# One scan for the four state sequences of a pair, the backward direction kept in scan order, output weights of power zero copied

## The reference

```python
for direction in range(2):
    lam_bar = jnp.exp(lam * dt)                      # complex, 32 groups x 64 states
    b_bar = ((lam_bar - 1.0) / lam)[..., None] * (b_re + 1j * b_im)
    order = (lambda t: t) if direction == 0 else (lambda t: jnp.flip(t, axis=1))
    bu_c = einsum('gpk,blgk->blgp', b_bar, order(uc))
    x_c = ssm_scan(lam_bar, bu_c)                    # x[t] = lam_bar * x[t-1] + bu[t]
    bu_l = einsum('gpk,blgk->blgp', b_bar, order(ul))
    bu_l = bu_l.at[:, 0].add(lam_bar * x_c[:, -1])   # latents go on from the context's last state
    x_l = ssm_scan(lam_bar, bu_l)
    ys_l += order(einsum('gkp,blgp->blgk', c_mat, x_l).real)
    ys_c += order(einsum('gkp,blgp->blgk', c_mat, x_c).real)
y = gelu(ys + d * u); y = y * sigmoid(y @ glu_w + glu_b)
```

## Time and profile before

| | |
|---|---|
| median of 3 runs | 1921.41 us (1920.11 to 1926.1) |
| the profiled execution | 1922.82 us, its span 1921.0 us |
| PE busy, share of the span | 1833.4 us, 95% |
| DVE | 1220.0 us, 64% |
| ACT | 728.3 us, 38% |
| POOL | 62.6 us, 3% |
| DMA | 257.81 MB, mean 134 GB/s |
| mean granted clock of PE | 0.969 |

### The profile page before, as it was taken

One profiled execution on the slowest core, in us unless ns is written; L12 is line 12 of the kernel. 1 busy time (PEld: TensorE's weight loads), 2 busy tenths in 40 slices (PEclk: granted clock), 3 DMA queues, 4 the chain that ended last, 5 costly groups with the idle time before them and its releaser, 6 DMA issues.

```text
span 1921.0 us, 25350 instructions
## 1 busy us (share of the span) xinstructions
PE 1833.4 (95%) x9680; PEld 1539.9 (80%) x9680; DVE 1220.0 (64%) x2020; ACT 728.3 (38%) x1003; POOL 62.6 (3%) x39
## 2 busy tenths in 40 slices
PE   6899999999889799999999999999999999989998
PEld 2688888877788587888888878888888797789998
DVE  4677677778999854777577357766333434755554
ACT  2522122336766833322132252312322434654343
POOL 0000000020000001000000100000002000010001
PEclk7999999999989998999999999999999999989999
DMA  7444545331110122554464235444223241034553
GB/s 298 154 175 157 188 183 209 120 113 66 45 45 28 39 72 104 186 202 148 148 235 146 94 129 192 172 153 178 95 77 113 107 176 55 2 111 174 179 183 120
DMA packets 39860, 257.81 MB, mean 134 GB/s; under 512 B 4688, under 2 KB 5840, under 8 KB 14832
## 3 DMA queue, kind: packets, MB, share of 16 engines
q1 hardware_dynamic: 39792, 256.92, 37.1%
HBM read 255.85 MB, written 1.05 MB: 134 GB/s over the span
## 4 chain that ended last, share of the span: by engine, by line
PE 84%; DVE 10%; ACT 3%; issue 2%; DMA 1%; SPq 0%; DVEq 0%; ACTq 0%
PE ps_all L1574 26%; PE ps_all L1578 25%; PE ps_all L1575 25%; DVE w_lo L924 2%; PE ps_all L1964 2%; PE bank L1622 1%; DMA start_scale<-in_w_scale 1%; PE bank L1977 1%; PE bank L2000 1%; ACT w_hi L538 1%; DVE cp L432 1%; DVE stat L1307 1%; PE bank L1789 1%; DVE wb L1238 0%; DVE normed L1294 0%
## 5 line engine op out<-in xcount | busy, mean ns | idle before, releaser
L1574 PE MATMUL ps_all<-a_hi,w_lo 128*128 128x512 f32 (+1 forms) x1800 | 663.4, 369 | 21.5 <-ACT a_hi L648 14.0
L1578 PE MATMUL ps_all<-a_lo,w_hi 128*128 128x512 f32 (+1 forms) x1800 | 657.4, 365 | 0.2 <-DVE a_lo L1063 0.2
L1575 PE MATMUL ps_all<-a_hi,w_hi 128*128 128x512 f32 (+1 forms) x1800 | 657.2, 365 | 0.0
L924 DVE TENSOR_TENSOR w_lo<-w_raw,w_hi 128x2048 fp32r<-128x2048 f32 (+3 forms) x184 | 376.5, 2046 | 162.1 <-ACT w_hi L538 160.9
L538 ACT ACTIVATE w_hi<-w_raw 128x2048 fp32r<-128x2048 f32 (+3 forms) x183 | 313.5, 1713 | 338.4 <-PE ps_all L1578 331.0
L1574 PEld LDWEIGHTS ps_all<-a_hi,w_lo 128*128 128x128 f32 x1800 | 345.5, 192 | 79.7 <-issue 16.2
L1578 PEld LDWEIGHTS ps_all<-a_lo,w_hi 128*128 128x128 f32 x1800 | 345.2, 192 | 56.8 <-DVE a_lo L1063 4.1
L1575 PEld LDWEIGHTS ps_all<-a_hi,w_hi 128*128 128x128 f32 x1800 | 345.8, 192 | 52.1 <-issue 0.2
L936 DVE SCALAR_TENSOR_TENSOR mod_junk<-mod_raw,cond 128x1024 bf16<-128x1024 f32 x256 | 302.7, 1220 | 5.4 <-ACT cond L566 2.7
L1574 PE MATMUL ps_all<-g_hi,w_lo 128*128 128x512 f32 (+1 forms) x704 | 258.4, 367 | 1.0 <-DVE w_lo L924 1.0
L1578 PE MATMUL ps_all<-g_lo,w_hi 128*128 128x512 f32 (+1 forms) x704 | 258.3, 367 | 0.0
(11 more groups left out here) (236 smaller groups left out, 1512.0 us busy)
## 6 DMA issues: line engine op xcount, KB each, us to landing
w_raw<-in_tiles SPq DMA_DIRECT2D x118, 1024.0 KB, 4.8
mod_raw<-in_w_mod SPq DMA_DIRECT2D x64, 1024.0 KB, 4.8
w_raw<-in_tiles SPq DMA_DIRECT2D x32, 768.0 KB, 4.1
w_raw<-in_tiles SPq DMA_DIRECT2D x32, 640.0 KB, 3.7
start_raw<-in_w_mod SPq DMA_DIRECT2D x4, 1024.0 KB, 16.1
start_scale<-in_w_scale SPq DMA_DIRECT2D x4, 1024.0 KB, 20.2
bias<-in_na_bias SPq DMA_DIRECT2D x2, 1536.0 KB, 8.9
cond<-in_cond SPq DMA_DIRECT2D x2, 1024.0 KB, 6.0
```

What stands on the lines that cost most here:

```text
L924: nc.vector.tensor_tensor(w_lo[:, slot, 0:size], w_raw[:, slot, 0:size], w_hi[:, slot, 0:size].bitcast(F32), ALU.subtract).then_inc(lo_rea ...
L1574: pe.matmul(dst, w[1], x[0], start=start, stop=False)
L1575: pe.matmul(dst, w[0], x[0], start=False, stop=False)
L1578: return pe.matmul(dst, w[0], x[1], start=False, stop=stop_)
```

## The change

- **Scans.** One `tensor_tensor_scan` over 512 elements does all four sequences of a pair. Its factors come from a new tile `rates` (two slots), which holds the rate of the direction in columns 1 to 127 of each sequence and zero in column 0, so that each sequence starts anew. POOL writes the zeros once, ACT writes the rest for each pair (`scan_rates`), and DVE waits for it.
- **Order of the backward direction.** For this the backward sequences have to lie in the order in which they are scanned. PE gets the blocks of `us` reversed within each half for the two backward products of `inputs_to_state`, and the backward states reversed in `outputs` (`in_scan_order`). The step numbers are then the same for both directions, and `const` is 128 columns narrower. `xs` is 129 columns for each sequence, with the padding in front.
- **States.** `turn_back` writes them with one instruction for each part instead of two.
- **Output weights.** `c_products` and `c_combine` do powers 1 to 4 only. Power zero is C itself (its imaginary part negated): ACT copies it into slots 0 and 9 (`present_outputs`), and `kernel_products` waits for that. All four products now lie in `prod`; `rates` takes the place of `cprod` and of a gap.

```diff
-    c[:, C_STEP:C_STEP + 2 * P] = np.concatenate(
-        [np.arange(1, P + 1), np.arange(64, 0, -1), np.arange(P, 64, -1)])
+    c[:, C_STEP:C_STEP + P] = np.arange(1, P + 1)
...
+                def present_outputs(b):
+                    act.wait_ge(S["pads"], 1)
+                    if b >= 2:
+                        act.wait_ge(S["y"], 2 * b - 2)
+                    for ri in range(2):
+                        for g in range(2):
+                            at = slice(64 * g, 64 * g + 64)
+                            ins = nc.scalar.activation(cp[at, b % 2, :, ri, 0::9, 16 * g:16 * g + 16],
+                                                       c_in[at, ri, 4 * b:4 * b + 4, :].rearrange("p (q d) k -> p q d k", d=2),
+                                                       ACT.Copy, scale=1.0 if ri == 0 else -1.0)
+                    ins.then_inc(S["present"], 1)
+                def scan_rates(pair):
+                    if pair >= 2:
+                        act.wait_ge(S["scan"], pair - 1)
+                    for d in range(2):
+                        ins = nc.scalar.activation(rates[:, pair % 2, d, :, 1:P],
+                                                   ones[:, 1:P].rearrange("p (a j) -> p a j", a=1).broadcast_to([P, 2, P - 1]), ACT.Copy,
+                                                   scale=r4[:, 2 * pair + d:2 * pair + d + 1])
+                    ins.then_inc(S["rates"], 1)
...
                 angles(0)
+                present_outputs(0)
+                scan_rates(0)
+                scan_rates(1)
                 split_hi(base + 1, 2048, 1)
...
                         angles(b + 1)
+                        present_outputs(b + 1)
                         turned(2 * b + 2)
                         turned(2 * b + 3)
...
+                    if b < 7:
+                        scan_rates(2 * b + 2)
                     gelu(2 * b)
                     if b < 7:
                         sines(b + 1)
+                        scan_rates(2 * b + 3)
...
-                    to = [prod[:, 320 * n:320 * n + 320] for n in range(2)] + [cprod[:, n] for n in range(2)]
+                    to = [prod[:, 256 * n:256 * n + 256] for n in range(4)]
...
-                    for ri in range(2):
-                        ins = nc.vector.tensor_tensor_scan(zs[:, 1, ri, 63::-1], r[1].broadcast_to([P, 64]),
-                                                           rot[:, 0, 1, ri, 63::-1], 0.0, mul, add)
-                    ins.then_inc(S["half"], 1)
-                    for ri in range(2):
-                        nc.vector.tensor_tensor_scan(zs[:, 0, ri, :], r[0].broadcast_to([P, P]),
-                                                     rot[:, 0, 0, ri, :], 0.0, mul, add)
-                    dve.wait_ge(S["half"], pair + 1)
-                    for ri in range(2):
-                        ins = nc.vector.tensor_tensor_scan(zs[:, 1, ri, 127:63:-1], r[1].broadcast_to([P, 64]),
-                                                           rot[:, 0, 1, ri, 127:63:-1], zs[:, 1, ri, 0:1], mul, add)
-                    ins.then_inc(S["scan"], 1)
+                    dve.wait_ge(S["rates"], pair + 1)
+                    nc.vector.tensor_tensor_scan(sq_acc[:], rates[:, slot].rearrange("p d r j -> p (d r j)"), scaled[:, 0],
+                                                 0.0, mul, add).then_inc(S["scan"], 1)
...
                     for ri, op in ((0, sub), (1, add)):
-                        at, to = ri * P + 63, ri * 130 + 65
-                        b = [back[:, n].rearrange("p d r j -> p (d r j)")[:, at:at + 194:193] for n in range(2)]
-                        nc.vector.tensor_tensor(flat[:, to:to + XS_D + 65:XS_D + 64], b[0], b[1], op)
-                        x_to = x[:, :, ri * 130:ri * 130 + 130].rearrange("p d (b j) -> p d b j", b=2)[:, :, :, 0:64]
-                        ins = nc.vector.tensor_tensor(x_to, back[:, 0, :, ri, :], back[:, 1, :, ri, :], op)
+                        ins = nc.vector.tensor_tensor(xs[:, pair % 2, :, ri, 1:P + 1], back[:, 0, :, ri, :], back[:, 1, :, ri, :], op)
...
+                nc.gpsimd.memset(rates[:, :, :, :, 0:1], 0.0)
...
+                def in_scan_order(x, d):
+                    return x.rearrange("p (b j) -> p b j", b=2)[:, :, ::-1] if d else x
...
-                        mm = pe.matmul(bank[1 + pair % 2][:, n * P:(n + 1) * P], vt[:, pair % 2, n, :], us_of(pair),
+                        mm = pe.matmul(bank[1 + pair % 2][:, n * P:(n + 1) * P], vt[:, pair % 2, n, :], in_scan_order(us[:, pair, :], n // 2),
...
                     pe.wait_ge(S["c"], b + 1)
+                    pe.wait_ge(S["present"], b + 1)
...
-                            x = xs[:, slot, XS_D * d + 130 * ri:XS_D * d + 130 * ri + 130].rearrange("p (b j) -> p b j", b=2)[:, :, d:d + 64]
-                            mm = pe.matmul(o, lhs, x, start=False, stop=(d == 1 and ri == 1))
+                            mm = pe.matmul(o, lhs, in_scan_order(xs[:, slot, d, ri, 0:P], d), start=False, stop=(d == 1 and ri == 1))
```

More of the change, by code:

```diff
@@ L75 @@
 COLUMNS = 2 * CHUNKS + 76
-XS_D = 262
 MAGIC = 1.5 * 2 ** 23
@@ L266, in program @@
                 prod = sbuf("prod", [P, 1024], F32, s5)
-                cprod = sbuf("cprod", [P, 2, 320], F32, s5)
-                sbuf("between", [P, 5632 - 4 * 1024 - 512 - 640], F32, s5)
+                rates = sbuf("rates", [P, 2, 2, 2, P], F32, s5)
                 c_in = sbuf("c_in", [P, 2, 32, 16], F32, s5)
@@ L326, in program @@
         s5_sem = {n: sem("s5_" + n) for n in (
-            "rows", "loads", "skip", "act", "tanh", "sin", "b", "pads", "us_act", "wprod", "w", "cprod", "c",
-            "ang", "magic", "frac", "abs", "tables", "turned", "vt", "v", "kmm", "k", "rot", "z", "half", "scan",
+            "rows", "loads", "skip", "act", "tanh", "sin", "b", "pads", "us_act", "wprod", "w", "cprod", "c", "present",
+            "ang", "magic", "frac", "abs", "tables", "turned", "vt", "v", "kmm", "k", "rot", "z", "rates", "scan",
             "back", "x", "y", "gelu")}
@@ L382, in program @@
         lgam = pt[:, 31, 0:8]
-        rates = cond_k[:].rearrange("p k v -> p (k v)")
-        lg = [pt[:, 31, 8 * n:8 * n + 8] for n in range(1, 4)] + [rates[:, 0:8], rates[:, 8:16], columns[:, C_COND:C_COND + 8]]
+        log_rates = cond_k[:].rearrange("p k v -> p (k v)")
+        lg = [pt[:, 31, 8 * n:8 * n + 8] for n in range(1, 4)] + [log_rates[:, 0:8], log_rates[:, 8:16], columns[:, C_COND:C_COND + 8]]
         prob = [scaled[:, 0], scaled[:, 1], normed[:, 0], normed[:, 1]]
@@ L422, in c_products @@
             for n, (p, z) in enumerate(x):
-                c = c_in[:, p, qd, :].rearrange("p c (a k) -> p c a k", a=1).broadcast_to([P, 4, 5, 16])
-                l = pows[:, z, qd, :].rearrange("p c (n a) -> p c n a", a=1).broadcast_to([P, 4, 5, 16])
-                ins = engine.tensor_tensor(to[n].rearrange("p (c n k) -> p c n k", c=4, n=5), c, l, ALU.mult)
+                c = c_in[:, p, qd, :].rearrange("p c (a k) -> p c a k", a=1).broadcast_to([P, 4, 4, 16])
+                l = pows[:, z, qd, :].rearrange("p c (n a) -> p c n a", a=1).broadcast_to([P, 4, 4, 16])
+                ins = engine.tensor_tensor(to[n].rearrange("p (c n k) -> p c n k", c=4, n=4), c, l, ALU.mult)
             return ins
@@ L431, in c_combine @@
                 at = slice(64 * g, 64 * g + 64)
-                ins = engine.tensor_tensor(cp[at, b % 2, :, ri, :, 16 * g:16 * g + 16],
-                                           of[0][at].rearrange("p (q n k) -> p q n k", q=2, n=10),
-                                           of[1][at].rearrange("p (q n k) -> p q n k", q=2, n=10), op)
+                ins = engine.tensor_tensor(cp[at, b % 2, :, ri, 1:9, 16 * g:16 * g + 16],
+                                           of[0][at].rearrange("p (q n k) -> p q n k", q=2, n=8),
+                                           of[1][at].rearrange("p (q n k) -> p q n k", q=2, n=8), op)
             return ins
@@ L1259, in rotate @@
                 def rotate(pair):
-                    c, slot = 2 * pair, pair % 2
+                    slot = pair % 2
                     v = bank[1 + slot][:].rearrange("p (d r j) -> p d r j", d=2, r=2)
-                    r = [r4[:, c + d:c + d + 1] for d in range(2)]
                     dve.wait_ge(S["v"], pair + 1)
@@ L1672, in state_rows @@
                     return x.rearrange("p n c -> p (n c)")
-                def us_of(pair):
-                    return us[:, pair, :]
+                def in_scan_order(x, d):
+                    return x.rearrange("p (b j) -> p b j", b=2)[:, :, ::-1] if d else x
                 def input_tile(j, part):
@@ L1750, in outputs @@
                         pe.wait_ge(S["gelu"], pair)
-                    pe.matmul(o, kt[:, b % 2, ql, :], us_of(pair), start=True, stop=False)
+                    pe.matmul(o, kt[:, b % 2, ql, :], us[:, pair, :], start=True, stop=False)
                     pe.wait_ge(S["x"], pair + 1)
```

23 lines of the change are left out of this document (10 added, 13 removed).

## The result

The changed kernel takes 1902.04 us (median of 5 runs, 1899.26 to 1904.9), the kernel before 1920.11 beside it (5 runs): a ratio of 0.9901, interval [0.9885, 0.9917]. Its profiled execution took 1899.26 us (span 1897.5, mean granted clock 0.976).

A forecast was written before the change was run, and what follows sets the result against it. DVE was taken to bound the first mixer's state-space loop: 12.0 us saved, less stalls of 0.3 and 0.5 and 0.8 for ACT's rates, gives 10.4 us, so 1911.0 us from 1921.4; range 1907.5 to 1916.5, about 85%.

The forecast's parts named there:

- The bound: State-space loop of the first mixer: DVE never stops from first rotation to last fraction, so time taken off shortens the span.
- The scan: DVE, each pair: one 512-wide scan takes 1.14 us to the next start instead of 1.62, saving 0.48 us.
- The copy: DVE's copy of the states, each pair: two wide instructions instead of four, saving 0.15 us.
- The output weights: DVE, each pass: products and combinations of 256 instead of 320 save 0.53 us; six passes count, 3.2 us.
- ACT: Rates cost 0.82 us a pair, mostly hidden; pair 15's lie in ACT's last run, 0.8 us on the path.
- DVE's waits for the tables: Loop passes 4 and 5: DVE stalls 0.13 us in each for ACT's tables, 0.3 us together.
- A: Rival: PE and ACT take over in passes 4 to 6, 3 to 5 us of gain gone, 1914 to 1916; 14%.
- B: Rival: backward reads slow PE's matmuls; at four times the cost, 1930 to 1931 us; 4%.
- C: Rival: a second streamed source doubles the scan's slope, scan 2.07 us, kernel 1923, no change; 5%.
- the dear end of the forecast: Loop scans: slope of 2.1 ns an element, a scan of 1.21 us; 1.4 us less gain, in the upper end.
- The rest of the kernel moves with it: Behind the exponential that ends the loop, each step is released by the one before, so the rest only shifts.
- a clock dip less on the path: Part of the range's lower end: one PE clock dip fewer on the path, 1.7 us.

The follow-up runs named there:

- e4: The kernel before with only the output-weights part of the change, scans and states as before: 1918.02 us, ratio 0.9978.
- e12: The changed kernel with four 128-wide scans and a broadcast rate in pairs 14 and 15, no ACT rates for them: 1902.65 us, ratio 0.9902.
- e13: The kernel before with constants of 960 columns and 112 columns behind the states, g_hi placed as in the changed kernel within 256 bytes: 1913.65 us, ratio 0.9961.
- e14: The kernel before with constants of 960 columns and 48 columns behind the states, g_hi at 52 within 256 bytes: 1913.61 us, ratio 0.9959.
- e3: The changed kernel with the constants and states tiles at their old widths (1088 and 1048 columns): 1910.33 us, ratio 0.9947.
- e7: The changed kernel with only the states tile back at 1048 columns: 1909.11 us, ratio 0.9938.
- e10: The changed kernel with 16 unused columns right ahead of g_hi: 1910.83 us, ratio 0.9941.
- e1: The kernel before, run again unchanged: 1921.30 us, ratio 1.0002.
- e2: The kernel before with the narrow constants tile (960 columns instead of 1088): 1923.54 us, ratio 1.0010.
- e9: The kernel before with the narrow constants tile and 16 unused columns behind the states: 1920.20 us, ratio 0.9993.
- e8: The changed kernel with four scans of 128 elements and a broadcast rate, no rates made by ACT: 1903.76 us, ratio 0.9917.
- e11: The changed kernel with 19 unused columns ahead of g_hi, which starts at a multiple of 128 bytes: 1910.62 us, ratio 0.9941.
- e6: The changed kernel with only the constants tile back at 1088 columns: 1904.38 us, ratio 0.9912.

## Why the prediction was wrong

**The bound, right.** DVE carried the loop, and what was taken from it came out of the span: the passes with rotary work went from 23.91 us to 22.35 (rotation to rotation, 531.94 to 554.29).

**The scan, mis-sized.** Forecast: 1.11 us, 1.14 with the start of the next. Measured: 1.22 and 1.26. The slope was drawn between two shapes that differ in direction too; the upper bound named there, twice the rate of an ordinary product, gave 1.21 and was right. The copy saves 0.14 for 0.15. By the passes with rotary work (1.56 us shorter, 0.53 of it the weights) a pair saves 0.52 us for 0.63: 14 x 0.11 = 1.5 us of the forecast weren't there. The rule of the Trainium skill, page "DVE: opcode table, instruction layouts, handler registers and perf-mode slots", section "Datapath and trigger behaviour", that the scan runs at half throughput, agrees with the trace: 2.15 ns an element against 1.05 for the product. The prediction had put what it would cost the loop at 1.4 us, and went by the slope.

**The output weights, right:** 0.53 us a pass, in the changed kernel (481.67 to 484.88, 3.21 for 3.74) and alone in e4.

**ACT, right.** The rates of a pair take 0.81 us to the next start (608.27 to 609.08) for 0.82 forecast; ACT's last run, from the start of the last tables to the exponential, went from 16.25 us (628.79 to 645.04) to 17.00 (610.78 to 627.78), 0.75 for 0.8 forecast, and e12 takes all of it back. DVE's waits for the tables were 0.23 us each for 0.13, two of them on the path as forecast, and for the weights 0.3 us for 0.5. The loop in the prediction's own terms: 14 x 0.52 + 6 x 0.53 - 0.5 - 0.3 - 0.75 = 8.9 us in place of 10.4.

**Rivals.** A fell: no pass is PE's, and its clock in 574 to 580 is 1.00. B fell with the 275 ns, C with the slope of 2.15 ns, which is the dear end of the forecast and not twice the slope.

**"The rest of the kernel moves with it": the step that failed.** It did more than move, in two ways.
- The place of `g_hi` and `g_lo`: 1584 x 4.4 ns = 7.0 us, shown by e13 and e14 without the change and by e3, e7 and e10 with it. The diff had `stat` from 1048 to 1032 columns in plain sight; the prediction gave this no cost and no bound, and so the range had no room for it. (Its lower end adds up to 1907.2, not 1907.5, which changes nothing.)
- PE's clock behind the loop. 60 us from the end of the loop, the granted clock was 0.89 before and is 0.94 after:

```profile
645.00:705.00 60.00, 54.21 (x222) 39.98 (x221) 38.31 (x65) 30.09 (x44) 0.00 (x0) 0.89 0.15 53
```
```profile
629.00:689.00 60.00, 54.27 (x234) 40.91 (x234) 38.32 (x65) 28.84 (x42) 0.00 (x0) 0.94 0.15 53
```

From the first exponential to the seventh `w_lo` behind it the traces of before, e1, e2, e4, e9, e13 and e14 take 107.0 to 107.5 us, the thirteen that scan as the change does (e8 and e12 among them) 102.7 to 107.3, 104.9 on average: 2.4 us less. Three of the thirteen (e7, e11, e12) have 107.1 to 107.3, so the change doesn't bring this every time. The prediction had this as "a clock dip less on the path (1.7)", in its lower end only. What decides whether a trace has that dip wasn't tried.

8.9 + 7.0 + 2.4 = 18.3 us, for 18.1 measured. That they agree to 0.2 us is in part luck: the 2.4 us are an average over single traces that differ by 4.6, and the opening isn't in the sum. For the same change with `g_hi` left where it was, 8.9 + 2.4 is 11.3, so 1909; e3, e7 and e10 measured 1909 to 1911.

**Open.** The opening, to the second `w_lo`, took 60.6 to 60.9 us in the five traces with wide constants, and 56.3 to 58.3 in eleven of the fifteen with narrow ones (60.1 to 60.7 in the others); the medians of e2 and e6 show no gain that can be told from none, so nothing is claimed. And why the place counts is open. The Trainium skill, page "SBUF — State Buffer", section "Who interferes with whom", has PE waiting for no other engine; no run here shows a collision with one, only that the same matmuls on the same operands go at 226.7 to 234.3 ns by where the moving operand starts. Only 0, 52, 84, 116, 128, 180 and 244 of 256 were tried, and 0 and 128 stand on a multiple of 16 where the others are 4 beyond one, so which places between them are quick isn't known. `a_hi` and `a_lo` stand at 60 in every kernel here, 8 bytes from the 52 of the changed one, and go at 226.7; but theirs are other blocks, so that is a hint and no test.

## What to carry to other kernels

Before costing an edit, list the tiles whose size it changes and those that come to lie elsewhere; if a stream of matmuls reads one of them, compare start-to-start distances there, since a shift of 64 bytes moved 1584 matmuls by 4.4 ns each. And when a gain comes out larger than its mechanism can give, build the change with the old layout, and the old kernel with the new one: that split 18 us into 11 and 7. For a primitive whose rate is uncertain, a bound from twice the rate of a plain product was nearer than a slope drawn through shapes that differ in something else.

## What the hardware showed that was not expected

- A matmul of 512 columns on split float32 operands goes at 226.7, 228.9, 233.3 to 233.4 or 234.3 ns from start to start at full clock, by the place of its moving operand within 256 bytes of a partition (244; 52; 0, 84, 116 and 180; 128). These are means of unequal steps: at 52 the three products of a tile go at 231.7, 226.0 and 229.1 ns, at 180 all at 233 to 234. All kernels run here fit, with either code.
- One scan of 512 elements takes 1224 ns, one of 128 takes 399, whether the rate is one broadcast value or a streamed row: 2.15 ns an element.
- The 128-column matmuls of the state inputs, half of which read their moving operand backward, take 275 ns in the median and 377 at most, as when all of them read forward, and the backward ones follow each other at the same 110 to 112 ns a record.
